# Norms across channels with one number per token on the partitions, and the third mixer's tail in another order

## What is computed

```python
def rms_norm(x, g):                       # across the channels of a token
    return x * lax.rsqrt(jnp.mean(x * x, axis=-1, keepdims=True) + EPS) * g

def layernorm(x, g, b):                   # second block's gating, third block's convolution
    xc = x - jnp.mean(x, axis=-1, keepdims=True)
    return xc * lax.rsqrt(jnp.mean(xc * xc, axis=-1, keepdims=True) + EPS) * g + b

# the end of the third block's mixer; attn and conv have 512 channels each
conv = silu(layernorm(dwconv(...), g_conv_ln, b_conv_ln))
mixed = concatenate([rms_norm(attn, g_out_attn), rms_norm(conv, g_out_conv)], axis=-1)
x = x + gt1 * (mixed @ w_out)
```

## Time and profile before

| | us |
|---|---|
| median of 3 runs | 3579.37 |
| lowest, highest | 3578.24, 3586.34 |
| the profiled execution | 3581.99 |
| its span from first to last instruction | 3580.2 |
| PE busy | 3275.2 (91%) |
| DVE, ACT, POOL busy | 1666.6, 1038.1, 1259.7 |
| mean granted clock of TensorE | 0.947 of full speed |

### The profile page before, as it was taken

The page is one execution under the profiler, slowest core; times in us unless marked ns, Lnnn a source line. Parts: engine busy times, 40 slices in busy tenths (PEclk is TensorE's granted clock), DMA queues, the critical chain, the costliest instruction groups (busy, mean ns, idle before and its releaser), DMA issues.

```text
span 3580.2 us, 62766 instructions
## 1 busy us (share of the span) xinstructions
PE 3275.2 (91%) x25656; PEld 2466.9 (69%) x25656; DVE 1666.6 (47%) x2427; ACT 1038.1 (29%) x1473; POOL 1259.7 (35%) x664
## 2 busy tenths in 40 slices
PE   8999999699899999999899998799987977779999
PEld 5757888568688877777577664388875633337887
DVE  5754552373455555773306105360514688526151
ACT  4413342222433334432232122222211311302121
POOL 3323444233233314444243220044432388003444
PEclk9999999899999999999999989999997985889999
DMA  3213333222000014554232210133321210012333
GB/s 127 83 30 94 94 98 102 71 72 75 2 3 3 3 42 147 186 179 146 65 114 76 77 59 30 41 100 95 99 84 48 71 41 1 0 47 83 100 94 100
DMA packets 73281, 266.94 MB, mean 75 GB/s; under 512 B 8255, under 2 KB 8282, under 8 KB 72912
## 3 DMA queue, kind: packets, MB, share of 16 engines
q1 hardware_dynamic: 72144, 260.81, 23.4%
q0 software_dynamic: 960, 3.60, 0.3%
HBM read 262.28 MB, written 2.10 MB: 74 GB/s over the span
## 4 chain that ended last, share of the span: by engine, by line
PE 73%; DVE 11%; issue 9%; POOL 4%; ACT 2%; DMA 0%; POOLq 0%; DVEq 0%; ACTq 0%; SPq 0%
PE gp L378 51%; PE gp L306 4%; PE gp L1146 4%; POOL w_low L349 3%; PE aux L516 3%; PE gp L2066 2%; DVE arena L2609 1%; PE aux L1263 1%; PE gp L1887 1%; PE aux L1146 1%; PE aux L1896 1%; PE gp L1889 1%; PE aux L1141 1%; DVE root L523 1%; ACT arena L586 0%
## 5 line engine op out<-in xcount | busy, mean ns | idle before, releaser
L349 POOL TENSOR_TENSOR w_low<-ring,w_high 128x1024 fp32r<-128x1024 f32 x397 | 953.6, 2403 | 1965.7 <-ACT w_high L318 1965.7
L318 ACT ACTIVATE w_high<-ring 128x1024 fp32r<-128x1024 f32 x397 | 419.8, 1059 | 1385.2 <-PE gp L378 1336.1
L378 PE MATMUL gp<-ffn_h,w_high 128*128 128x512 f32 x2432 | 759.7, 394 | 26.3 <-DVE ffn_h L399 25.0
L378 PEld LDWEIGHTS gp<-ffn_h,w_high 128*128 128x128 f32 x2432 | 456.0, 189 | 138.7 <-issue 23.5
L378 PE MATMUL gp<-ffn_h,w_low 128*128 128x512 f32 x1216 | 475.8, 391 | 0.0
L378 PE MATMUL gp<-ffn_high,w_high 128*128 128x512 f32 x928 | 362.0, 390 | 2.8 <-POOL w_low L349 2.7
L378 PE MATMUL gp<-ffn_low,w_high 128*128 128x512 f32 x864 | 336.8, 390 | 0.0
L378 PE MATMUL gp<-ffn_high,w_low 128*128 128x512 f32 x864 | 336.7, 390 | 0.0
L378 PEld LDWEIGHTS gp<-ffn_h,w_low 128*128 128x128 f32 x1216 | 229.7, 189 | 48.2
L378 PE MATMUL gp<-in_h,w_high 128*128 128x512 f32 x768 | 240.8, 395 | 10.7 <-DVE in_h L399 10.7
L1994 DVE TENSOR_TENSOR arena<-arena 128x512 f32<-128x512 f32 x64 | 152.5, 2383 | 202.4 <-ACTq L162 202.4
(11 more groups left out here) (440 smaller groups left out, 5318.7 us busy)
## 6 DMA issues: line engine op xcount, KB each, us to landing
ring<-in_weights SPq DMA_DIRECT2D x438, 512.0 KB, 3.6
H<-in_ada SPq DMA_DIRECT2D x48, 512.0 KB, 4.3
X<-in_x SPq DMA_DIRECT2D x4, 512.0 KB, 8.2
out_x<-X SPq DMA_DIRECT2D x8, 256.0 KB, 4.3
arena<-in_sm POOLq DMA_DIRECT2D x1, 1024.0 KB, 5.0
cst<-in_cst SPq DMA_DIRECT2D x1, 756.0 KB, 9.9
arena<-in_hy_f_w POOLq DMA_DIRECT2D x1, 512.0 KB, 5.1
arena<-in_hy_delta POOLq DMA_DIRECT2D x1, 512.0 KB, 5.6
```

The source lines that it names most:

```text
L318: nc.scalar.activation(w_high[:, slab % PARTS, :], ring[:, slab % RING, :], ACT.Copy).then_inc(high_ready, 1)
L349: nc.gpsimd.tensor_tensor(w_low[:, slab % PARTS, :], ring[:, slab % RING, :], w_high[:, slab % PARTS, :], ALU.subtract).then_inc(low_ready, 1)
L378: last = nc.tensor.matmul(gp[:, t.bank, :], wt[:, slab % PARTS, w], x(k), start=(k == 0 and q == 0), stop=(k == sum(kt) - 1 and q == 2))
```

## The change

`norm_pe` becomes two functions. `stat_pe` takes the squared tile as the weights: four blocks of 128 tokens, each a product of the block (128x128) with two columns of ones (128x2). So each squared tile takes four products instead of one, and the sums come out as one number per token, tokens on the partitions, in 8 columns of the bank. ACT takes the square root of 128x4 numbers (`stat_act`) and DVE inverts 128x4 (`invert_dve`). `root_pe` then spreads them: four products per norm, each with one column of `root` repeated 128 times as the weights and the identity as the moving side (128x128), into the same bank of `aux`. DVE's scalar_tensor_tensor reads that bank in place of `root` (`ROOT`). Since the spread root lives in the bank until the last tile is scaled, `stat_pe` and `sum_pe` also wait for `root_used`, told by DVE behind the last scaling. The three norms between large products keep the products of ones (`sums_pe`). `centre_dve` subtracts the mean straight from the bank, one scalar_tensor_tensor per tile, and ACT's copy is gone.

The third mixer's tail is ordered anew on PE, ACT and DVE (`out3_pe` on PE): the convolution's sum; the attention output's sums and root, in bank 1; the convolution's variance and root; out3's products of its first four tiles with the attention half of the input (16 products); the convolution output's sums and root; then the other 48 products. ACT squares the attention's output right behind its copies, into four tiles of their own, and each of its copies now settles before it is told.

```diff
 
+        inv_ready, root_ready, root_used = sem("f_dec"), sem("f_comb"), sem("dft_ready")
+        ROOTS0 = 8
+
         class Count:
...
@@ -497,19 +500,71 @@
             return base + per * t.j if t.it is None else t.it * (per * t.body) + (base + per * t.j)
 
 
-        def norm_act(act, a, n, src, sq, src_wait, scale, eps="eps", root_wait=None):
+        def ROOT(bank=0):
+            return aux[:, bank, :]
+
+        def tok_root(bank, b=None):
+            at = 16 + 8 * bank
+            return root[:, at:at + 4] if b is None else root[:, at + b:at + b + 1]
+
+        def stat_pe(pe, n, sq, bank=0):
+
+            if n_pe.sums:
+                pe.wait_ge(stat_ready, n_pe.sums)
+            if n_pe.roots:
+                pe.wait_ge(root_used, ROOTS0 + n_pe.roots)
+            for k in range(n):
+                n_pe.sq += 1
+                pe.wait_ge(sq_ready, n_pe.sq)
+                for b in range(4):
+                    last = nc.tensor.matmul(aux[:, bank, 2 * b:2 * b + 2], sq(k)[:, b * P:(b + 1) * P], ones[:, 0:2],
+                                            start=(k == 0 and b == 0), stop=(k == n - 1), skip_group_check=True)
+            last.then_inc(sum_ready, 1)
+            n_pe.sums += 1
+
+        def root_pe(pe, bank=0):
+
+            n_pe.roots += 1
+            pe.wait_ge(inv_ready, ROOTS0 + n_pe.roots)
+            for b in range(4):
+                last = nc.tensor.matmul(aux[:, bank, b * P:(b + 1) * P], tok_root(bank, b).broadcast_to((P, P)), ident,
+                                        start=True, stop=True)
+            last.then_inc(root_ready, 1)
+
+        def stat_act(act, scale, eps="eps", bank=0):
+
+            n_act.sums += 1
+            act.wait_ge(sum_ready, n_act.sums)
+            nc.scalar.activation(tok_root(bank), aux[:, bank, 0:8:2], ACT.Sqrt, scale=scale,
+                                 bias=const(eps)).then_inc(stat_ready, 1)
+
+        def invert_dve(dve, v, bank=0):
+
+            n_dve.sums += 1
+            dve.wait_ge(stat_ready, n_dve.sums)
+            v.go(nc.vector.reciprocal(tok_root(bank), tok_root(bank)))
+            v.tell(inv_ready)
+
+        def root_wait_dve(dve):
+
+            n_dve.roots += 1
+            dve.wait_ge(root_ready, ROOTS0 + n_dve.roots)
+
+        def norm_act(act, a, n, src, sq, src_wait, scale, eps="eps"):
             for k in range(n):
                 src_wait(k)
                 nc.scalar.activation(sq(k), src(k), ACT.Square).then_inc(sq_ready, 1)
-            n_act.sums += 1
-            act.wait_ge(sum_ready, n_act.sums)
-            if root_wait:
-                root_wait()
-            nc.scalar.activation(root[:], aux[:, 0, :], ACT.Sqrt, scale=scale, bias=const(eps)).then_inc(stat_ready, 1)
+            stat_act(act, scale, eps)
 
...
+        def sums_pe(pe, n, sq):
             if n_pe.sums:
                 pe.wait_ge(stat_ready, n_pe.sums)
+            if n_pe.roots:
+                pe.wait_ge(root_used, ROOTS0 + n_pe.roots)
             for k in range(n):
                 n_pe.sq += 1
                 pe.wait_ge(sq_ready, n_pe.sq)
@@ -517,13 +572,20 @@
             last.then_inc(sum_ready, 1)
             n_pe.sums += 1
 
+        def scale_dve(dve, v, n, src, gain, dst, done, bank=0):
+            root_wait_dve(dve)
+            for k in range(n):
+                ins = nc.vector.scalar_tensor_tensor(out=dst(k), in0=src(k), scalar=gain(k), in1=ROOT(bank),
+                                                     op0=ALU.mult, op1=ALU.mult)
+                if k < n - 1:
+                    ins.then_inc(done, 1)
+                else:
+                    v.go(ins)
+                    v.tell(done, root_used)
+
...
@@ -1837,32 +1899,29 @@
         def sum_pe(pe, n, src):
 
             pe.wait_ge(stat_ready, n_pe.sums)
+            pe.wait_ge(root_used, ROOTS0 + n_pe.roots)
             for k in range(n):
                 last = nc.tensor.matmul(aux[:, 0, :], ones, src(k), start=(k == 0), stop=(k == n - 1))
             last.then_inc(sum_ready, 1)
             n_pe.sums += 1
 
-        def mean_act(act, width):
-            n_act.sums += 1
-            act.wait_ge(sum_ready, n_act.sums)
-            nc.scalar.activation(root[:], aux[:, 0, :], ACT.Copy, scale=1.0 / width).then_inc(stat_ready, 1)
-
-        def centre_dve(dve, v, n, src):
+        def centre_dve(dve, v, n, src, width):
 
             n_dve.sums += 1
-            dve.wait_ge(stat_ready, n_dve.sums)
+            dve.wait_ge(sum_ready, n_dve.sums)
             for k in range(n):
-                v.go(nc.vector.tensor_tensor(src(k), src(k), root[:], ALU.subtract))
-            v.tell(ln_c)
+                v.go(nc.vector.scalar_tensor_tensor(out=src(k), in0=aux[:, 0, :], scalar=-1.0 / width, in1=src(k),
+                                                    op0=ALU.mult, op1=ALU.add))
+            v.tell(stat_ready, ln_c)
 
         def scale_shift_dve(dve, v, n, src, gain, bias, dst, done):
 
-            n_dve.sums += 1
-            dve.wait_ge(stat_ready, n_dve.sums)
-            v(nc.vector.reciprocal(root[:], root[:]))
+            root_wait_dve(dve)
             for k in range(n):
-                v(nc.vector.scalar_tensor_tensor(out=dst(k), in0=src(k), scalar=gain(k), in1=root[:],
+                v(nc.vector.scalar_tensor_tensor(out=dst(k), in0=src(k), scalar=gain(k), in1=ROOT(),
                                                  op0=ALU.mult, op1=ALU.mult))
+                if k == n - 1:
+                    dve.sem_inc(root_used, 1)
                 nc.vector.tensor_scalar(dst(k), dst(k), bias(k), None, ALU.add).then_inc(done, 1)
 
 
...
 
         def post_norm_dve(dve, v, gain):
-            n_dve.sums += 1
-            dve.wait_ge(stat_ready, n_dve.sums)
-            v(nc.vector.reciprocal(root[:], root[:]))
+            invert_dve(dve, v)
+            root_wait_dve(dve)
             for k in range(DT):
                 o = arena[:, k, :]
-                v(nc.vector.scalar_tensor_tensor(out=o, in0=o, scalar=pcol(gain, k), in1=root[:],
+                v(nc.vector.scalar_tensor_tensor(out=o, in0=o, scalar=pcol(gain, k), in1=ROOT(),
                                                  op0=ALU.mult, op1=ALU.mult))
+                if k == DT - 1:
+                    dve.sem_inc(root_used, 1)
                 nc.vector.tensor_tensor(X[:, k, :], X[:, k, :], o, ALU.add).then_inc(x_ready, 1)
             n_dve.x += DT
 
...
@@ -2156,10 +2216,8 @@
                                           ACT.Gelu_apprx_tanh if bU <= t.j < bCX else ACT.Copy))
                 a.tell(drained[t.bank], in2_ready)
             norm_act(act, a, 2, arena_tiles(bCQ), bsq, lambda k: None, 1.0 / 256)
-            norm_act(act, a, 1, arena_tiles(bCKV), arena_tiles(bOUT + 2), lambda k: None, 1.0 / 128,
-                     root_wait=lambda: act.wait_ge(lat_ready, 2))
-            act.wait_ge(lat_ready, 3)
-            mean_act(act, 256)
+            norm_act(act, a, 1, arena_tiles(bCKV), arena_tiles(bOUT + 2), lambda k: None, 1.0 / 128)
+            n_act.sums += 1
             norm_act(act, a, 2, arena_tiles(bV), arena_tiles(bOUT + 3), lambda k: act.wait_ge(ln_c, 1), 1.0 / 256)
...
+            out3_pe(pe)
             norm_pe(pe, DT, Hk)
             ffn2_pe(pe, 3)
 
-        def norm_pe_at(pe):
-
+        def out3_pe(pe):
+
+            st = STAGE["out3"]
+            tiles = list(loop_tiles(pe, st))
+
+            def products(t, ks):
+                for i in ks:
+                    last = nc.tensor.matmul(gp[:, t.bank, :], ring[:, (st.slab0 + t.j) % RING, i * P:(i + 1) * P],
+                                            arena[:, dAT + i, :], start=(i == 0), stop=(i == DT - 1))
+                return last
+
+            pe.wait_ge(cv_ready, CONV_DONE)
             pe.wait_ge(dsa_out, 4)
-            pe.wait_ge(cv_ready, 5)
             sum_pe(pe, 4, arena_tiles(dCV))
-            norm_pe(pe, 4, arena_tiles(46))
-            norm_pe(pe, 4, arena_tiles(46))
-            norm_pe(pe, 4, arena_tiles(46))
+            stat_pe(pe, 4, arena_tiles(42), 1)
+            root_pe(pe, 1)
+            stat_pe(pe, 4, arena_tiles(46))
+            root_pe(pe)
             pe.wait_ge(an_ready, 4)
+            for t in tiles[0:RING]:
+                bank_wait(pe, t)
+                slab_wait(pe, st.slab0 + t.j)
+                products(t, range(4))
+            stat_pe(pe, 4, arena_tiles(46))
+            root_pe(pe)
             pe.wait_ge(cn_ready, 4)
+            for t in tiles[0:RING]:
+                products(t, range(4, DT)).then_inc(slab_done, 1)
+            for t in tiles[RING:]:
+                bank_wait(pe, t)
+                slab_wait(pe, st.slab0 + t.j)
+                products(t, range(DT)).then_inc(slab_done, 1)
 
...
             for i in range(4):
-                nc.scalar.activation(arena[:, dAT + i, :], aux[:, i, :], ACT.Copy).then_inc(dsa_out, 1)
-            mean_act(act, 512)
+                a.go(nc.scalar.activation(arena[:, dAT + i, :], aux[:, i, :], ACT.Copy))
```

(48 more changed lines are left out.)

14 lines of the change are left out of this document (7 added, 7 removed).

## The result

| | before | changed |
|---|---|---|
| median of 6 runs, us | 3582.11 | 3607.12 |
| lowest, highest | 3577.68, 3593.08 | 3599.30, 3611.46 |
| profiled execution | 3581.99 | 3599.30 |
| its span, mean clock | 3580.2, 0.947 | 3597.4, 0.935 |

The changed kernel takes 1.0066 times the time before (95% interval 1.0047 to 1.0085): 25.0 us by the medians. It is slower, as forecast, and 3607.12 lies 1 us from the 3606 forecast.

What follows compares the result with a forecast made beforehand. The prediction took PE, busy 91% of the span, to bound the kernel. Its terms summed to +26.2 us, 3608.2 against the profiled 3581.99; as that execution lay 2.6 above the median, it forecast 3606, range 3590 to 3620.

Steps and rivals of the forecast that it cites:

- (a) to (d): Dearer sums: norms behind wide products +14.8 us, out2's result +4.8, ahead of in3 +3.9, waits for the bank +20.9.
- (a): Four norms straight behind wide products: sums from 7.03 to 10.75 us each, together +14.8; bounds +0.2 and +6.9 each.
- (d): Norms ahead of in2 and the second feed-forward part: sums wait for the previous norm's last scaling, together +20.9 us.
- The rival with the full clock: Whole kernel: the clock stays full under narrow products, -38 us, 3541; chance 4%.
- The rule on weight loads: Loads in the sums: columns divided by 1.2, in ns, 107 for 128 columns; 64 loads 6.8 us at either clock level.
- (e): Square root, reciprocal and spread: 2.7 us from sums' end to first scaling instead of 4.14; over the norms -12.2 us.
- (f): Latents' statistics: spreads on PE and sums waiting for scalings start the large product 6.6 us later; +7.0 with cold running.
- (g): Third mixer's tail: one of three norms' latencies hides behind a quarter of out3, -13.0 us; bounds -6 and -25.

## Why the forecast was right, point by point

- **Narrow products lose the clock** ((a) to (d)). Forecast from the earlier trace rows: 10.5 to 10.75 us per norm behind wide products. Measured 10.82, 8.62, 11.08 and 11.14. Only the final norm did better: the clock fell 5.5 us into its sums, and 3.1 us into those ahead of RWKV. Behind out2 11.22 (11.9 forecast), ahead of in3 13.79 (14.0). That the width is the cause, and not the loads or their number, the run with 128 columns shows.
- **The rival with the full clock** failed by its condition, and its price was too high as well. It had -38 us and 3541; the run with 128 columns, which comes nearest to the condition, had -21 and 3562. There too the clock was at half behind idle time: the latents cost +6.0 where the rival had 0, the sums ahead of in3 took 10.04 us and not 7.2.
- **The rule on weight loads** of the Trainium skill ("TensorE: Matmul & The Clock Gate", "LDWEIGHTS (loading the stationary operand)"), which the prediction names beside that rival, is near these traces at the full level (0.107 us by the rule, 0.114 per record) and not at the half (0.215).
- **The wait for the bank** ((d), +20.9). First scaling to the sums' end 19.4 and 24.4 us, where 19.6 and 24.5 stood in the forecast; taking the wait away gave back 10.7 us, where 12 were expected.
- **The shorter root** ((e)). Measured 2.74 us from the sums' end to the first scaling (2.7). From the sums' end to in2's first product 8.0 (7.9), ahead of the third block's feed-forward part 9.1 where it was 11.2: 2.1 less, where I took 1.5.
- **The latents** ((f)). Counted from the first sums, the large product starts 5.8 us later; 6.6 was forecast, and +7.0 with a cold start behind it, which cost nothing in the trace.
- **The tail** ((g), -13.0). From the sum to out3's end -14.7, less 0.8 by which the sum starts later: -13.9. The attention sums took 4.91 us and not 6.5, for the clock was still full when they began.
- **The sum and luck.** The forecast had +26.2 us, the medians gave +25.0. The stretches of the table that hold norms add up to +22.3 in the traces, and the whole of the traces to +17.2. Single terms are off by up to 2.2, in both directions. So the mechanism is borne out term by term, to some 2 us each; that the total came within 1.2 us is partly luck, and when the clock falls in a norm differs from one execution to the next.
- **Slips in the working.** The chain of (g) gives the attention sums 6.5 us, where 32 records at its own 0.217 are 6.9; the rival with the full clock has (a) +1.2, where its own bound of 0.2 for each of four norms gives 0.8. Neither moves a total by more than 0.4.

## What to carry to other kernels

Before wide products are replaced by narrow ones, look in the trace for narrow ones of the same kernel and read the granted clock over their whole length: here two such stretches gave the cost of the sums behind wide products to within 0.4 us for three norms of four, and missed the fourth by 2. A result that moves from SBUF into an accumulation bank turns each of its readers into something that the next accumulation waits for; here a second bank took that wait away. And a change of two parts is worth measuring in its parts: the order of the tail was worth 18 us on its own while the norms alone lost 31. The two don't simply add up: by these figures both together would lose 13, and they lost 25. Nor was the idea of the norms what lost: with 128 columns and banks of their own the new norms reached 3538.42, where the old norms in the new order had 3564.94.

## What the runs showed of the hardware that I had not expected

- 64 records of 128x128 by 128x128 in float32 took 7.30 us, and 64 of 128x128 by 128x2 at the same full clock would take 7.2 by the earlier trace rows (an estimate; 32 of them took 3.63 in the tail, and 32 with 128 columns 3.73). Between 2 and 128 moving columns the width cost next to nothing here, and behind wide products the clock stayed at 1.00 through the wide form while it fell to 0.50 in the narrow one.
- A norm that starts behind idle time is not lost: ahead of in3 the 64 records with 128 columns took 10.04 us, and the clock rose within them; with 2 columns they took 13.79, all at half.
- A shorter wait between small steps seems to have paid twice: with 1.7 us of waiting less ahead of the key-value sums the clock was full in three steps, which took 3.8 us less. This is read from single traces; the medians, 9.6 us apart where 2 to 3 were expected, point the same way.
